# A fixed first expert: its weights loaded during the second block, its rows gathered inside the router

## The reference, cut to what matters

```python
mod = (c @ w_ada[l] + b_ada[l])[:, None, :]
sh1, sc1, gt1, sh2, sc2, gt2 = jnp.split(mod, 6, axis=-1)
h = rms_norm(x, g_mix[l]) * (1.0 + sc1) + sh1
x = x + gt1 * parallel_mixer(h, ...)
h = rms_norm(x, g_ffn[l]) * (1.0 + sc2) + sh2
x = x + gt2 * moe_ffn(h, ...)
return rms_norm(x, g_final)

# moe_ffn, for each token the four experts with the largest logits, gates = softmax of those four:
gu = xb @ w_gu[e] + b_gu[e]                      # [rows, 2048]
gate = jnp.minimum(gu[:, :1024], 7.0)
up = jnp.clip(gu[:, 1024:], -7.0, 7.0)
y = ((up + 1.0) * gate * sigmoid(1.702 * gate)) @ w_down[e] + b_down[e]
out[token] += y * gate_of(token, e)
```

## Time and profile before

| | |
|---|---|
| time, median of 3 runs | 2186.51 us (2185.75 to 2186.84) |
| the profiled execution, its own time | 2185.5 us |
| its span | 2183.7 us |
| PE busy | 2041.9 us, 94% |
| DVE, ACT, POOL busy | 603.3, 311.7, 64.8 us |
| mean granted TensorE clock over the span | 0.967 |
| DMA, moved | 599.77 MB, mean 275 GB/s |
| second block starts, router, items | about 1005 us; 1130 to 1157 us; 1156 to 2170 us |

### The profile page before, as it was taken

The page is one execution under the profiler, slowest core; times in us unless marked ns, Lnnn a source line. Parts: engine busy times, 40 slices in busy tenths (PEclk is TensorE's granted clock), DMA queues, the critical chain, the costliest instruction groups (busy, mean ns, idle before and its releaser), DMA issues.

```text
span 2183.7 us, 24406 instructions
## 1 busy us (share of the span) xinstructions
PE 2041.9 (94%) x9982; PEld 1161.7 (53%) x9982; DVE 603.3 (28%) x1192; ACT 311.7 (14%) x700; POOL 64.8 (3%) x68
## 2 busy tenths in 40 slices
PE   8988999999988999999788999999999999999996
PEld 7766588848766688846644333333333333333332
DVE  0467443402367430003632111111111111111112
ACT  1325110001334210002410000000000000000001
POOL 0022000000022000000010000000000000000000
PEclk9979999999989999999987999999999999999999
DMA  7430088854330045444007999999999999999996
GB/s 303 149 116 1 1 308 307 342 227 155 124 122 26 20 186 210 154 167 164 39 8 315 429 428 428 428 429 428 429 428 428 430 428 429 428 429 428 428 428 260
DMA packets 43823, 599.77 MB, mean 275 GB/s; under 512 B 4992, under 2 KB 5296, under 8 KB 7888
## 3 DMA queue, kind: packets, MB, share of 16 engines
q1 hardware_dynamic: 43760, 598.87, 66.9%
HBM read 597.78 MB, written 1.07 MB: 274 GB/s over the span
## 4 chain that ended last, share of the span: by engine, by line
PE 69%; DMA 23%; DVE 6%; ACT 1%; issue 1%; SPq 0%; ACTq 0%; DVEq 0%
DMA ring<-in_stream 23%; PE ps L1849 14%; PE ps L1240 14%; PE ps L1261 7%; PE ps L376 6%; PE ps L1876 3%; PE ps L390 2%; PE ps L1167 2%; PE ps L1831 2%; PE ps L1926 2%; PE ps L1838 2%; PE ps L1611 1%; PE ps L1450 1%; PE ps L777 1%; PE ps L789 1%
## 5 line engine op out<-in xcount | busy, mean ns | idle before, releaser
L1849 PE MATMUL ps<-ring,HT 128*64 128x512 f32 x2176 | 487.8, 598 | 10.7 <-DMA ring<-in_stream 10.7
L1849 PEld LDWEIGHTS ps<-ring,HT 128*64 128x64 f32 x2176 | 147.6, 137 | 325.0 <-issue 276.5
L1240 PE MATMUL ps<-XT,ring 128*128 128x256 f32 (+1 forms) x1536 | 305.9, 362 | 3.3 <-DVE XT L313 3.3
L1240 PEld LDWEIGHTS ps<-XT,ring 128*128 128x128 f32 x1536 | 271.9, 190 | 36.8 <-DVE XT L313 3.7
L1876 PE MATMUL ps<-ring,HT 128*64 128x512 f32 x1088 | 247.7, 598 | 33.9 <-DMA ring<-in_stream 33.0
L1876 PEld LDWEIGHTS ps<-ring,HT 128*64 128x64 f32 x1088 | 72.6, 136 | 196.1 <-issue 121.6
L1261 PE MATMUL ps<-ring,HT 128*128 128x512 f32 x352 | 151.7, 592 | 0.0
L376 PE MATMUL ps<-XT,ring 128*128 128x256 f32 x576 | 124.7, 379 | 1.5 <-DMA ring<-in_stream 1.5
L1984 DVE TENSOR_SCALAR HT<-ps 128x512 f32<-128x512 f32 x34 | 23.5, 692 | 352.1 <-PE ps L1849 352.1
L376 PEld LDWEIGHTS ps<-XT,ring 128*128 128x128 f32 x576 | 109.3, 190 | 16.4 <-issue 1.7
L1261 PEld LDWEIGHTS ps<-ring,HT 128*128 128x128 f32 x352 | 66.7, 190 | 82.4 <-issue 82.3
(11 more groups left out here) (398 smaller groups left out, 1814.0 us busy)
## 6 DMA issues: line engine op xcount, KB each, us to landing
ring<-in_stream SPq DMA_DIRECT2D x278, 2048.0 KB, 14.6
SB<-in_ln SPq DMA_DIRECT2D x8, 512.0 KB, 9.4
SB<-mod_rows SPq DMA_DIRECT2D x1, 3072.0 KB, 9.7
CST<-in_const SPq DMA_DIRECT2D x1, 1362.0 KB, 5.4
...
X<-in_x SPq DMA_DIRECT2D x1, 1024.0 KB, 5.0
...
```

Source lines behind the costliest of these rows:

```text
L1240: m = pe.matmul(ps[:, 2 * (f % 2) + a, j * T + cols.start:j * T + cols.stop], w[:, k, a, j * P:(j + 1) * P], XT[:, k, cols], start=k == 0, ...
L1849: m = pe.matmul(ps[HD * half:HD * (half + 1), a, :], XE[:, 2 * b + k, q * SLOTS_E:(q + 1) * SLOTS_E], w[:, k, a, half, :], start=False, st ...
```

## The change

- The first item is always expert 0, in whichever way the tokens fall: its number of rows is taken as at least one. With that, its six slots have fixed addresses. SP loads them during the second block: b 4 first, b 0 and b 1 when the projections have freed their ring slots, b 2 and b 3 after the output projection, b 5 after the residual. `b_down` and `b_gu` are loaded there too.
- The two down slots get two buffers of their own in `SB` (`MOE_BUF`), beside the four of the ring. Each later load waits until its own buffer's last content has been used, which is the sixth use before it (for the very last item's two down slots the second).
- In the router, DVE makes item 0's one-hot directly from the ranks, and PE gathers item 0's rows alone (32 records of 64 columns), before it turns the gates and sums the owners; then come item 0's biases and its first gate/up slot, before the places. The rest follows in `moe_pe`: slot 1, the gather of item 1 alone, slots 2 and 3, and only then the product of gates and `b_down`.
- The gate vector `MOD[5]` is applied in item rows: POOL multiplies `b_down` by it and copies its second half beside the first for partitions 64 to 127 (`gated_pool`), and `moe_rows_dve` multiplies instead of copying. `final_dve` has only the add left, for each tile as soon as PE has returned that tile; the signalling transpose is gone. ACT uses its square root once before the last turn. The output is stored by two DMAs, one for each tile.
- The modulation rows that are needed (2 to 5) are read back by four DMAs of 512 KB each to four places, instead of one of 3072 KB.

```diff
-        MOD = view(SB, 4096, [6, D])
+        MOD = {2: view(SB, 2 * D, [D]), 3: view(SB, 4096, [D]), 4: HN[:].rearrange("p a b -> p (a b)"),
+               5: TOK[:].rearrange("p t n -> p (t n)")}
...
-        BD = view(SB, 2 * D, [D])
+        BD = view(SB, D, [D])
...
+            sp.dma_start(BD[0:NE, :], dram["b_down"]).then_inc(S("par2_loaded"), 16)
+            moe_first_load(sp, 4)
+            for b in range(2):
+                sp.wait_ge(S("proj2_ready"), 6 + 2 * b)
+                moe_first_load(sp, b)
+            sp.wait_ge(S("nsa_out"), DEPTH + 1)
+            sp.dma_start(BGU[0:NE, :, :, :].rearrange("p h a n -> p (h a n)"), dram["b_gu"]).then_inc(S("par2_loaded"), 16)
+            sp.wait_ge(S("mix2_ready"), NT)
+            for b in range(2, 4):
+                moe_first_load(sp, b)
+            sp.wait_ge(S("x_ready"), 2 * DEPTH + 1)
+            moe_first_load(sp, 5)
...
         def modulation_rows_sp(sp):
-            sp.wait_ge(S("mod_turned"), 1)
-            sp.dma_start(dram["mod_rows"], MT).then_inc(S("mod_saved"), 16)
-            sp.wait_ge(S("mod_saved"), 16)
-            sp.dma_start(MOD.rearrange("p m d -> p (m d)"),
-                         dram["mod_rows"].rearrange("k p -> (k p)").unsqueeze(0).broadcast_to([P, 6 * D])).then_inc(S("mod_rows"), 16)
+            sp.wait_ge(S("mod"), 2)
+            sp.dma_start(dram["mod_rows"], MT).then_inc(S("mod_rows"), 16)
+            sp.wait_ge(S("mod_rows"), 16)
+            rows = dram["mod_rows"].rearrange("(m k) p -> m (k p)", m=6)
+            for m, to in MOD.items():
+                sp.dma_start(to, rows[m:m + 1, :].broadcast_to([P, D])).then_inc(S("mod_rows"), 16)
...
+        def gated_pool(pool):
+
+            pool.wait_ge(S("x_ready"), 2 * DEPTH + 1)
+            pool.wait_ge(S("h_rows"), 2 * NT)
+            nc.gpsimd.tensor_copy(MOD[5][HD:P, 0:512], MOD[5][HD:P, 512:1024]).then_inc(S("h_rows"), 1)
+            pool.wait_ge(S("par2_loaded"), 64)
+            pool.wait_ge(S("h_rows"), 2 * NT + 1)
+            nc.gpsimd.tensor_tensor(BD[0:NE, :], BD[0:NE, :], MOD[5][0:NE, :], ALU.mult).then_inc(S("h_rows"), 1)
...
-            if t == NT - 1:
-                v.sem_inc(S("moe_slot"), RING)
...
+        BGU = view(SA, 0, [2, 2, 512])
...
+            pe.matmul(ps[:, 6, 0:NE], strict, SEL[:, 0, :], start=True, stop=True)
...
-            pe.matmul(ps[0:NE, 0, P:P + 1], cst("pairs")[0:NE, P:P + NE], NXT, start=True, stop=True).then_inc(S("item_end"), 1)
+            pe.matmul(ps[0:NE, 6, P:P + 1], cst("pairs")[0:NE, P:P + NE], NXT, start=True, stop=True).then_inc(S("item_end"), 1)
...
             m.then_inc(S("rank_t_ps"), 1)
+            pe.wait_ge(S("moe_p"), 1)
+            pe.wait_ge(S("h_rows"), 2 * NT)
+            moe_gather_one_pe(pe, 0)
             pe.wait_ge(S("gates"), 1)
             for t in range(NT):
-                m = pe.transpose(ps[0:NE, 1, t * P:(t + 1) * P], GT2[:, t, :], ident)
+                m = pe.transpose(ps[0:NE, 7, t * P:(t + 1) * P], GT2[:, t, :], ident)
             m.then_inc(S("gates_t_ps"), 1)
             pe.wait_ge(S("owner"), 1)
-            pe.matmul(ps[0:1, 0, 256:256 + NITEM], cst("part")[0:NE, :], OH, start=True, stop=True)
-            m = pe.matmul(ps[0:1, 0, 384:384 + NITEM], ones[0:NE, 0:1], OH, start=True, stop=True)
+            pe.matmul(ps[0:1, 6, 256:256 + NITEM], cst("part")[0:NE, :], OH, start=True, stop=True)
+            m = pe.matmul(ps[0:1, 6, 384:384 + NITEM], ones[0:NE, 0:1], OH, start=True, stop=True)
             m.then_inc(S("owner_ps"), 1)
 
+            pe.wait_ge(S("moe_xe"), 1)
+            pe.wait_ge(S("par2_loaded"), 64)
+            moe_bias_pe(pe, 0)
+            moe_gate_up_pe(pe, 0, 0, 0, (0,))
...
+        def moe_bias_down_pe(pe):
+
+            pe.wait_ge(S("h_rows"), 2 * NT + 2)
+            pe.wait_ge(S("moe_xe"), 2)
             for t in range(NT):
                 for c in range(2):
                     pe.matmul(ps[:, 4 + 2 * t + c, :], GTT[0:NE, t * P:(t + 1) * P], BD[0:NE, c * 512:(c + 1) * 512],
...
+            I(nc.vector.tensor_scalar(EOW[0:NE, 0, :], cst("ones")[0:NE, 0:SLOTS_E], ident[0:NE, 0:1], None, ALU.mult))
...
-            L(nc.vector.tensor_copy(TOT, ps[0:NE, 1, 2 * NE:2 * NE + 1]))
+
+            L(nc.vector.tensor_tensor(TOT, ps[0:NE, 6, 2 * NE:2 * NE + 1], ident[0:NE, 0:1], ALU.max))
 
             L(nc.vector.tensor_scalar(OVER, cst("iota")[0:NE, 0:T // SLOTS_E], float(SLOTS_E), TOT, ALU.mult, ALU.is_lt))
             nc.vector.tensor_reduce(NXT, OVER, AX.X, ALU.add).then_inc(S("nxt"), 1)
             v.wait_ge(S("nxt"), 1)
+            for t in range(NT):
+                ins = nc.vector.tensor_scalar(EP0[:, t, 0, :], cst("iota")[:, 0:SLOTS_E], 2000.0, RNK[:, t, 0:1],
+                                              ALU.add, ALU.is_equal)
+                if t < NT - 1:
+                    I(ins)
+            ins.then_inc(S("moe_p"), 1)
...
+        MOE_BUF = [slot(S_MOE + b) for b in range(RING)] + [view(SB, at, [SLOT]) for at in (6080, 10176)]
+        moe_arrived = [arrived[(S_MOE + b) % RING] for b in range(RING)] + [S("moe_down_low"), S("moe_down_high")]
+
+        def moe_first_load(sp, b):
+
+            sp.dma_start(MOE_BUF[b], dram["stream"][S_MOE + b]).then_inc(moe_arrived[b], 16)
+
+        def moe_load(sp, i, b, freed):
+
+            sp.wait_ge(S("moe_slot"), freed)
+            sp.dma_start(MOE_BUF[b], dram["stream"][bass.ds(i * ITEM_SLOTS + S_MOE + b, 1), :, :]
+                         .rearrange("a p n -> (a p) n")).then_inc(moe_arrived[b], 16)
...
         def moe_sp(sp):
-            sp.wait_ge(S("h_ready"), 2)
-            sp.dma_start(BD[0:NE, :], dram["b_down"]).then_inc(S("par2_loaded"), 16)
-            sp.dma_start(BGU[0:NE, :, :, :].rearrange("p h a n -> p (h a n)"), dram["b_gu"]).then_inc(S("par2_loaded"), 16)
             last = moe_last_pair(sp)
-            first = sp.value_load(ITI[0:1, 8:9], min_val=0, max_val=NE - 1)
+            e = sp.value_load(ITI[0:1, 9:10], min_val=0, max_val=NE - 1)
             for b in range(4):
-                moe_load(sp, 0, b, first, b)
+                moe_load(sp, e, b, b + 1)
             with sp.Fori(0, last) as it:
                 for q in range(2):
-                    moe_step_sp(sp, it, q, True)
-            moe_step_sp(sp, last, 0, True)
-            moe_step_sp(sp, last, 1, False)
-
-        def moe_step_sp(sp, it, q, more):
-            if more:
-                e = moe_expert(sp, it * 2 + q + 1)
-                for b in range(4):
-                    moe_load(sp, it, moe_use(q, b), e, b)
-            e = moe_expert(sp, it * 2 + q)
+                    e = moe_expert(sp, it * 2 + q + 2)
+                    for b in range(4):
+                        moe_load(sp, e, b, it * PAIR_SLOTS + 6 * q + 5 + b)
+                    e = moe_expert(sp, it * 2 + q + 1)
+                    for b in range(2):
+                        moe_load(sp, e, 4 + b, it * PAIR_SLOTS + 6 * q + 9 + b)
+            e = moe_expert(sp, last * 2 + 1)
             for b in range(2):
-                moe_load(sp, it, moe_use(q, 4 + b) - (0 if more else 4), e, 4 + b)
-
-
-        def need_moe_slot(pe, it, at):
-            i = S_MOE + at
-            pe.wait_ge(arrived[i % RING], it * (16 * PAIR_SLOTS // RING) + 16 * (i // RING + 1))
+                moe_load(sp, e, 4 + b, last * PAIR_SLOTS + 9 + b)
...
+        def need_moe_slot(pe, it, q, b):
+            before = (S_MOE + b) // RING if b < RING else 0
+            pe.wait_ge(moe_arrived[b], it * 32 + 16 * (before + q + 1))
...
+        def moe_gather_one_pe(pe, q):
+
+            for k in range(KT):
+                for t in range(NT):
+                    m = pe.matmul(ps[:, 4 + q, k * SLOTS_E:(k + 1) * SLOTS_E], HF[:, t, k * P:(k + 1) * P], EP0[:, t, q, :],
+                                  start=t == 0, stop=t == NT - 1)
+            m.then_inc(S("moe_xe_ps"), 1)
...
-                pe.wait_ge(S("moe_p"), it + 2)
+                pe.wait_ge(S("moe_p"), it + 3)
             moe_bias_pe(pe, 1 - q)
-            moe_gate_up_pe(pe, it, moe_use(q, 0), 1 - q, (0, 1))
+            moe_gate_up_pe(pe, it, q + 1, 1 - q, (0, 1))
...
         def moe_pe(pe):
+            moe_gate_up_pe(pe, 0, 0, 0, (1,))
+            pe.wait_ge(S("moe_p"), 2)
+            moe_gather_one_pe(pe, 1)
+            moe_gate_up_pe(pe, 0, 0, 0, (2, 3))
+            moe_bias_down_pe(pe)
             last = moe_last_pair(pe)
-            pe.wait_ge(S("moe_p"), 1)
-            pe.wait_ge(S("h_rows"), 2 * NT)
-            for half in range(2):
-                moe_gather_pe(pe, 0, half, 2 + half)
-            pe.wait_ge(S("moe_xe"), 2)
-            pe.wait_ge(S("moe_gu_evac"), 1)
-            moe_bias_pe(pe, 0)
-            moe_gate_up_pe(pe, 0, 0, 0, range(4))
             with pe.Fori(0, last) as it:
                 moe_step_pe(pe, it, 0, True)
                 moe_step_pe(pe, it, 1, False)
             moe_step_pe(pe, last, 0, False)
             moe_turn_pe(pe, last, 1)
```

(50 more changed lines are left out.)

88 lines of the change are left out of this document (42 added, 46 removed).

## The result

The changed kernel takes 2175.82 us, median of 20 runs, beside 2185.49 for the kernel before in as many: a ratio of 0.9959, 95% interval 0.9949 to 0.9970, so 9 us faster (6.5 to 11). The forecast was 2166: the sign is right and the time lies inside the range, near its upper end, but 9 us were gained where 20 were forecast. The profiled execution took 2176.1 us with a span of 2174.3; the prediction's sum for that span is 2183.7 - 15.7 - 5.1 = 2162.9. The 11.4 us between the two are what the rest of this document accounts for.

A forecast was written before the change was run, and what follows sets the result against it. The prediction took the loop to be set by DMA bytes and its start by PE. From 2185.5 it took 15.7 for earlier loads and 5.1 for the end, 2164.7; the median's 1.0 more gave 2165.7, rounded to 2166, range 2157 to 2177.

The forecast's parts named there:

- what sets the loads: Start of the loop: PE using slot 0 releases item 1's first load, 12.5 us after the first load of before.
- the item table: Router: the table moves to about 1160, 5.8 us later, which costs nothing because loads wait for used slots.
- rival (c): Loop: up to six transfers in flight make each slot dearer; at 3% it costs 28 us, 2194; chance 0.05.
- rival (d): Start: PE doesn't hold item 1's loads, so #202 lands 28 us earlier, 2153; chance 0.03.
- (a): Router: the clock rises during the first gather and the rest runs at full rate, 2162.5; chance 0.22.
- The end: After the last return: earlier adds and the split output save 5.1 us, between 3.8 and 6.
- the clock would be back soon after slot 0 had begun: Base case at item 0's first gate/up slot: full-height work raises the clock, slot 0 takes 5.3 us; chance 0.47.
- Nothing elsewhere: Outside start, loop and end: modulation reads, POOL's two new operations and the second block's loads cost 0.
- Step 4 of the second item's loads: PE's work from places to item 1's slot 0, including gates x b_down 3.5 and biases 1.9, ends at 1192.7.
- I charge 0.7 in total: Loads behind #11: requests at most half a microsecond late until about 1225, then never; 0.7 us in total.
- The last item's down slots: End of the loop: they land 11.4 us after #201 and #202, PE needs the second at 11.7; cost 0, at worst 1.
- The deeper lead: Loop: a lead of six slots for four gives nothing where the rate is the bound.

The follow-up runs named there:

- e5: Changed kernel with the gates' transposes and the owner sums ahead of the first gather: 2177.61 us, ratio 0.9957 to the kernel before.
- e2: Changed kernel with POOL's product on the down biases held until the router's first one-hot: 2174.26 us, ratio 0.9952 to the kernel before.
- e6: Changed kernel with the end as before the change, without POOL's down-bias product: 2177.04 us, ratio 0.9957 to the kernel before.
- e9: Changed kernel with POOL's product late, last item's down slots in ring buffers, down-bias product between slots 2 and 3, no filler matmuls: 2176.80 us.
- e1: Changed kernel with the last item's two down slots loaded into ring buffers 0 and 1: 2174.20 us, ratio 0.9943 to the kernel before.
- e3: Changed kernel with nine filler matmuls on PE in the router's waits: 2167.72 us, ratio 0.9926 to the kernel before.
- the control: The changed kernel itself, timed once more beside its variants: 2176.48 us, ratio 0.9963 to the kernel before.
- e4: Changed kernel with a load lead of four slots in place of six: 2186.10 us, ratio 1.0004 to the kernel before.
- e7: Changed kernel with the down-bias product moved between item 0's slots 2 and 3: 2175.53 us, ratio 0.9951 to the kernel before.

## Why the prediction was partly right

**Right: what sets the loads.** PE's arrival at slot 0 releases item 1's loads, 13.8 us after the first load of before (forecast 12 to 13; the rest is point 1 below). The first gather took 6.74 us (6.5), the item table came at 1160.4 (about 1160), its delay cost nothing (e5), 198 loads are addressed by the table, the loop kept its rate, which refutes rival (c), and rival (d) fell with the first load at 1169.58. The clock stayed at 0.50 through the first gather, so (a) didn't come. The end measured 10.48 us from the last return's start, before 15.5: 5.0 saved for 5.1 forecast, with the last half of the output landing 2.6 us after its issue (forecast 2.7; the 0.41 MB/us in that term stands in no row, and the loop's 428 GB/s gives nearly the same). The 3.2 us that the prediction worked out from the Trainium skill did not come; the section it names is on the gpsimd path, and these DMAs are issued by SP. That the clock would be back soon after slot 0 had begun held roughly: it came 4.9 us after (1168.2), so that slot 0 took 6.02 us for 5.3.

**Wrong by 11.4 us of span, in four steps:**

1. *"Nothing elsewhere ... POOL's two new operations: 0."* I asked when POOL's result is wanted (at 1184) and not what its running does to DVE beside it, which is on PE's path. The row of the changed kernel has 2.35 us for 0.17, and the router was 40.75 us long for 38.0. Of these 2.8 us, 2.2 are that instruction and 0.7 slot 0's. With POOL's product out of the way (e2, e6, e9) the router is 2.8 us shorter. In the profile the blocks ahead of the router happened to end 1.6 us earlier than before (1128.83 for 1130.47), so only 1.1 us of it shows in the absolute time of the first load. The contention I did weigh, DMA against DVE, was the wrong pair.
2. *Step 4 of the second item's loads, "gates x b_down 3.5, biases 1.9".*
3. *"I charge 0.7 in total"* for holes behind #11: from its landing to #202's 937.9 us passed, where 191 x 4.896 is 935.1. That is 2.8 for 0.7, of which 1.2 fell on the last item alone (#196 to #202 took 30.6 us, 29.4 in e1, but 29.5 also in e3, whose last loads are the changed kernel's; what took it isn't shown).
4. *The last item's down slots, "0, at worst 1".* I took 7.8 us from issue to landing for both, the value of a load into an idle queue. But #204 was issued while #203 was under way, and took 9.99 and, in the control, 9.09. The DMA share of 0.23 from 2140 to 2143, ahead of both, shows that the line had run dry by then. PE waited 2.03 us, and in the first profile the slot ran at half clock after that wait (5.35 for 3.65). 4.0 us in that execution; 1.4 in the control; 0 in e1.

Together 1.1 + 4.1 + 2.1 + 4.0 = 11.3 of the 11.4, for the one execution that was profiled. The second fall of the clock, 3.3 us of it, is the part whose cause stays open.

For point 1 the trace of the kernel before had the warning: beside DVE's add POOL's product took 3.21 us, for the 2.35 of the earlier trace rows when alone, and the add 1.46 for 1.22:

```profile
1133.70 1.46 DVE L1634 TENSOR_TENSOR X<-X,SB 128x1024 f32<-128x1024 f32 x1
...
1134.17 3.21 POOL L1417 TENSOR_TENSOR SA<-SA,SB 128x1024 f32<-128x1024 f32 x1
```

**Wrong without a price in the sum:** *"The deeper lead (six for four) gives nothing where the rate is the bound."* e4 refutes it: without the deeper lead the changed kernel is level with the old one. The sentence is true of the loop and false of the start, where the rate isn't the bound; my own sum used the six-slot lead there ("the requests come with the lead of six slots") without noticing that it was what made the sum come out.

**What the times can't tell.** Over the changed kernel's 20 runs the time goes with the mean granted clock (0.960 to 0.969, correlation -0.84) and spreads over 17 us. Edits worth 1 to 3 us (e1, e2) are shown by records that repeat in every trace with the same code, and agree with the medians; they are not shown by them. The gain of e7 is shown by neither. What made the clock fall earlier or later in one execution than in the next, from the same code, stays open.
